# The norms' inverse roots on ScalarE as logarithm and exponential, and a weight cast in quarters between squares

## The chip, the cores and the metric

The kernel runs on one core of a Trainium2 chip. The core has TensorE (matrix products into PSUM), VectorE and GpSimd (elementwise work), ScalarE (activation functions and copies) and SyncE, which here only issues transfers; each engine runs its own list of instructions in order, and they meet through semaphores. The metric is the device time of one execution in microseconds: the median of three runs is 2175.29 us (2175.22 to 2176.02).

## The reference

Two blocks follow each other. The first prepends 16 learned tokens to 256 positions of width 1024 and runs two layers of feed-forward, token mixer and feed-forward, each followed by a layer norm:

```python
def layer_norm(x, g, b):
    mu = jnp.mean(xf, axis=-1, keepdims=True)
    var = jnp.mean(jnp.square(xf - mu), axis=-1, keepdims=True)
    return ((xf - mu) * lax.rsqrt(var + LN_EPS) * g + b)
...
h = layer_norm(h, ln_in_g, ln_in_b)
for l in range(DEPTH):
    h = layer_norm(ALPHA * h + 0.5 * swiglu_ffn(h, ...), ...)
    h = layer_norm(ALPHA * h + token_mix(h, ...), ...)
    h = layer_norm(ALPHA * h + 0.5 * swiglu_ffn(h, ...), ...)
```

`token_mix` joins windowed means, a gated causal convolution with a layer norm inside, and a retention with a group norm per head. The second block takes the result with 256 context positions through two layers whose norms are of another kind:

```python
def rms_norm(x, g):
    y = xf * lax.rsqrt(jnp.mean(xf * xf, axis=-1, keepdims=True) + EPS)
    return y * g
...
x = x + g1 * rms_norm(mixer(modulate(rms_norm(x, g0), ...)), g1n)
x = x + g2 * rms_norm(conv_ffn(modulate(rms_norm(x, g2n), ...)), g3n)
```

Its even layer mixes with a windowed attention and a bidirectional mLSTM, its odd layer with latent attention, whose query and key ranks have an rms_norm each. The context goes through the even layer alone. All of it is float32. Every `rsqrt` here is one of the roots that the change rewrites, but for the one per head in the mLSTM's output (HSTD), which is computed as logarithm and exponential already.

## The kernel before, in words

The activations lie transposed: 128 channels on the partitions, eight tiles of 1024 channels, and positions along the free axis (272 in the first block, 2 x 256 in the second). A weight matrix comes in units of 128x2048 into four slots of a ring (RAW). A product in float32 is made of three products of shorter numbers: the weight is split into a rounded part WHI (`high`, a cast on ScalarE, line 1484) and a remainder WLO (`rest`, a subtraction on VectorE, line 2080), the input likewise into XHI and XLO, or XB and its remainder; TensorE multiplies high by high, low by high and high by low. `high(n)` waits until unit n has landed and its slot's parts are free.

The order of the work on each engine is written out by hand, one function per engine and stage; semaphores with counted values join them. No scheduler reorders it.

A layer norm of the first block runs so. The last output tiles of a feed-forward come out of TensorE one after the other. VectorE adds the residual (PL, line 2162), ScalarE squares (`square_tiles`, SLF, line 1518), VectorE and GpSimd sum squares and tiles, TensorE sums over the channels with a matrix of ones, ScalarE squares the mean (DSQ), VectorE forms the variance (VAR, line 2202), ScalarE takes the square root (RSTD, line 1527), VectorE inverts it (`invert`, line 2132) and scales PL (line 2119), ScalarE writes XHI and X (lines 1492, 1494), VectorE the remainder XLO (line 2126). Meanwhile TensorE runs `keep_busy`: matrix products of ones with no user (fillers in the text). q counts these norms from 0 to 5; q=0, 2, 3 and 5 end a feed-forward (`ffn1`), q=1 and 4 end a mixer. At q=0, 2 and 3 the next stage's second unit is cast on ScalarE behind the root; at q=5 between two squares.

In the second block an input norm squares X (SQ), sums on TensorE (`in_stat`), takes the root into RSTD for the latents or RSC for the context (`in_root`, line 1711), inverts it (`in_recip`, line 2425) and forms PRE and XB (`in_tiles`, lines 2436 and 2441; `in_hi`, line 1716). An output norm (`y_square`, `y_root`, line 1725) ends in `post`, which inverts (line 2461), scales PRE and adds it to X. In the mixers there are CSTD (the convolution's norm, inverted at line 2376) and GSTD (the group norm, line 2395, which TensorE spreads over the partitions); in the odd layer DQSTD and CKSTD (lines 2747 and 2753).

ScalarE holds one set of activation tables at a time. Where the next activation's function isn't in it, an ACT_TABLE_LOAD stands ahead of it; a one-element activation into DUMMY was used to bring a load forward.

Of the kernel before, what the change touches and what calls it, by code (L numbers as in the profile page):

```python
# [20 lines left out]
CT = D // P  # L21
# [50 lines left out]
def build(nc, A, out):  # L72
    with ExitStack() as ctx:
# [40 lines left out]
        DUMMY = small.put("DUMMY", [1])  # L114
# [197 lines left out]
        def conv_at(i, f):  # L312
# [18 lines left out]
        ln_centred, ln_std, ln_rstd, ln_scaled = sem("ln_centred"), sem("ln_std"), sem("ln_rstd"), sem("ln_scaled")  # L331
# [23 lines left out]
        def halves(name):  # L355
            return [sem(f"{name}{z}") for z in range(2)]

        in_sq, norm_power, norm_std, in_scaled, in_high, in_low = (
            halves("in_sq"), halves("norm_power"), halves("norm_std"), halves("in_scaled"), halves("in_high"),
            halves("in_low"))  # L360
# [15 lines left out]
        odd_done, odd_taken, odd_mm, odd_std, odd_step = (  # L376
            sem("odd_done"), sem("odd_taken"), sem("odd_mm"), sem("odd_std"), sem("odd_step"))
# [295 lines left out]
        def _(pe):  # L673
# [141 lines left out]
            def mixer(l):  # L815
# [76 lines left out]
                pe.wait_ge(cv_std, l + 1)  # L892
# [38 lines left out]
                pe.wait_ge(gn_rstd, l + 1)  # L931
# [96 lines left out]
            def even_inputs():  # L1028
# [6 lines left out]
                pe.wait_ge(norm_std[0], in_at(0))  # L1035
                pe.wait_ge(ln_std, 7)
                half_unit(EVEN0 + 2, 0, 4)
                pe.wait_ge(norm_std[1], in_at(0))
# [220 lines left out]
            def ffn_both():  # L1259
# [3 lines left out]
                pe.wait_ge(norm_std[1], in_at(1))  # L1263
# [30 lines left out]
                for z in (1, 0):  # L1294
                    for j in range(CT):
# [8 lines left out]
                        if z == 0 and j == 7:  # L1304
                            pe.wait_ge(norm_std[1], y_at(1))
# [10 lines left out]
            def odd_inputs():  # L1316
# [38 lines left out]
                for n in range(4):  # L1355
# [10 lines left out]
                    if n == 0:  # L1366
                        pe.wait_ge(odd_taken, 2)
                        pe.wait_ge(norm_std[1], in_at(2))
                        mm(pe, PS[:, 3, :], ONES[:, 2, :], CKSQ[:, :], True, True).then_inc(odd_mm, 1)
                        pe.wait_ge(tab_loaded, RT_LOADED)  # L1370
                        pe.wait_ge(odd_std, 1)
# [97 lines left out]
        def _(act):  # L1469
# [15 lines left out]

            def norm_out(e, gain, bias):
# [11 lines left out]
            def input_norm():  # L1498
                act.wait_ge(start_set, N_SET)
                act.activation(DUMMY[:, :], EPS5[:, :], ACT.Sqrt)  # L1500
# [8 lines left out]
                act.activation(RSTD[:, 0:L1], PS[:, 5, 0:L1], ACT.Sqrt, bias=EPS5[:, 0:1]).then_inc(ln_std, 1)  # L1509
# [10 lines left out]
            def norm(q, behind_root=lambda: None):  # L1520
# [6 lines left out]
                act.activation(RSTD[:, tk], VAR[:, tk], ACT.Sqrt, bias=EPSH[:, 0:1]).then_inc(ln_std, 1)  # L1527
                behind_root()
# [9 lines left out]
            def ffn1(l, b):  # L1538
# [42 lines left out]
                act.activation(DUMMY[:, :], EPSH[:, :], ACT.Sqrt)  # L1581
                square_tiles(q, SLF, range(3, 4))
                if q == 5:
                    high(u0 + FFN_STEPS + 1)
                square_tiles(q, SLF, range(4, CT))
                norm(q, (lambda: None) if q == 5 else (lambda: high(u0 + FFN_STEPS + 1)))

            def mixer(l):
# [74 lines left out]
                act.activation(CSTD[:, :], PS[:, 1, 0:L1], ACT.Sqrt, bias=EPS5[:, 0:1]).then_inc(cv_std, 1)  # L1663
# [11 lines left out]
                act.activation(GS[:, 2:4, :], PS[:, 2:4, 0:L1], ACT.Silu).then_inc(gs_done, 1)  # L1675
                act.wait_ge(gn_var, l + 1)
                act.activation(GSTD[:, :], PS[:, 4, 0:L1], ACT.Sqrt, bias=EPS5[:, 0:1]).then_inc(gn_std, 1)
# [1324 lines left out]
```

## Time and profile before

| | us |
|---|---|
| median of three runs (lowest to highest) | 2175.29 (2175.22 to 2176.02) |
| profiled execution: span, first to last instruction | 2171.1 |
| time of the profiled execution outside its span | not listed |
| median of the runs less the span | 4.2 |
| TensorE busy | 2110.9 (97%) |
| VectorE busy | 1571.7 (72%) |
| ScalarE busy | 1054.7 (49%) |
| GpSimd busy | 156.5 (7%) |
| mean granted TensorE clock, share of full speed | 0.994 |

PE is TensorE's matrix products, DVE VectorE, ACT ScalarE, POOL GpSimd. A busy share is an average over stages with different limits; what an edit is worth is read where it stands, from the wait that ends last there. A table load on ScalarE takes 1.283 us, and there are 33.

### The profile page before, as it was taken

What the parts mean: (1) busy time and instruction counts of PE and PEld (TensorE: products, weight loads), DVE (VectorE), ACT (ScalarE), POOL (GpSimd) and SP (SyncE); (2) the same over time, 40 slices, a digit from 0 to 9 for tenths busy, and PEclk for the clock granted to TensorE, in tenths of its full rate; (3) what the DMA queues carried; (4) which work ended last, traced back from release to release, by engine and by line L of the source; (5) the groups of instructions that cost most, each with busy time, mean ns of one, the idle gap of its engine ahead of it and who ended that gap; (6) DMA issues with size and microseconds to landing.
All of it is one profiled execution on the core that took longest, in us unless ns stands there. A gap on an engine that the chain in (4) does not pass through costs nothing.

```text
span 2171.1 us, 35296 instructions
## 1 busy us (share of the span) xinstructions
PE 2110.9 (97%) x14830; PEld 1928.9 (89%) x14830; DVE 1571.7 (72%) x2374; ACT 1054.7 (49%) x1551; POOL 156.5 (7%) x195
## 2 busy tenths in 40 slices
PE   9999999999999999999999988999999999999997
PEld 8999989999999998999897774898888888579997
DVE  7878998878988798998852667466556346858774
ACT  6443656443644465644552446345445234746653
POOL 1201102201200101200100000000000001100000
PEclk9999999999999999999999999999999999999999
DMA  7665526666566543777331120113222222123552
GB/s 293 224 239 191 211 92 262 233 239 248 211 235 245 205 156 119 273 276 254 126 120 54 59 96 9 58 61 117 97 97 96 98 78 100 37 78 118 189 179 97
DMA packets 48334, 334.93 MB, mean 154 GB/s; under 512 B 5612, under 2 KB 6716, under 8 KB 8880
## 3 DMA queue, kind: packets, MB, share of 16 engines
q1 hardware_dynamic: 38384, 267.47, 34.7%
q0 software_dynamic: 9792, 65.21, 8.0%
q8 instruction: 117, 1.92, 0.4%
q14 instruction: 41, 0.34, 0.0%
HBM read 331.61 MB, written 1.05 MB: 153 GB/s over the span
## 4 chain that ended last, share of the span: by engine, by line
PE 84%; DVE 9%; ACT 3%; issue 2%; DMA 1%; POOL 1%; DVEq 0%; ACTq 0%; POOLq 0%
PE PS L468 83%; ACT WHI L1484 1%; PE PS L1214 1%; DVE WLO L2080 1%; DVE PRE L2436 1%; POOL SUM L571 1%; DVE RSTD L2132 1%; DVE XB L2441 0%; DVE STAT L2648 0%; DVE PL L2194 0%; DVE PL L2121 0%; DMA RAW<-in_up_a 0%; DMA RAW<-in_mix 0%; DVE TM L2595 0%; ACT PR L1895 0%
## 5 line engine op out<-in xcount | busy, mean ns | idle before, releaser
L2080 DVE TENSOR_TENSOR WLO<-RAW,WHI 128x2048 fp32r<-128x2048 f32 (+1 forms) x251 | 572.4, 2285 | 214.1 <-ACT WHI L1484 211.4
L468 PE MATMUL PS<-XB,WHI 128*128 128x256 f32 (+1 forms) x3136 | 702.1, 320 | 6.7 <-DVE XB L2441 2.4
L1484 ACT CAST WHI<-RAW 128x2048 fp32r<-128x2048 f32 (+1 forms) x251 | 474.9, 1895 | 283.3 <-DMA RAW<-in_dn_c 78.1
L468 PEld LDWEIGHTS PS<-XB,WHI 128*128 128x128 f32 x3136 | 523.0, 191 | 51.3 <-issue 8.9
L468 PE MATMUL PS<-XHI,WHI 128*128 128x272 f32 (+1 forms) x1760 | 497.9, 289 | 4.2 <-ACT XHI L1492 4.2
L468 PE MATMUL PS<-XB,WLO 128*128 128x256 f32 (+1 forms) x1568 | 498.0, 318 | 0.0
L468 PE MATMUL PS<-XHI,WLO 128*128 128x272 f32 (+1 forms) x1760 | 489.4, 287 | 0.0
L468 PE MATMUL PS<-XLO,WHI 128*128 128x272 f32 (+1 forms) x1760 | 481.2, 287 | 2.3 <-DVE XLO L2126 2.3
L468 PEld LDWEIGHTS PS<-XHI,WHI 128*128 128x128 f32 x1760 | 328.3, 188 | 8.2 <-issue 7.1
L468 PEld LDWEIGHTS PS<-XLO,WHI 128*128 128x128 f32 x1760 | 322.2, 188 | 4.1 <-DVE XLO L2126 3.6
L468 PEld LDWEIGHTS PS<-XHI,WLO 128*128 128x128 f32 x1760 | 325.7, 188 | 0.0
L468 PEld LDWEIGHTS PS<-XB,WLO 128*128 128x128 f32 x1568 | 299.5, 191 | 20.1
L468 PE MATMUL PS<-GHI,WHI 128*128 128x272 f32 (+1 forms) x704 | 200.1, 286 | 0.0
L468 PE MATMUL PS<-GHI,WLO 128*128 128x272 f32 (+1 forms) x704 | 199.7, 285 | 0.0
L2491 DVE SCALAR_TENSOR_TENSOR AC<-CB,FCW,AC 128x512 f32<-128x512 f32 (+1 forms) x176 | 97.1, 614 | 131.5 <-ACT AC L1742 103.8
L468 PE MATMUL PS<-GLO,WHI 128*128 128x272 f32 (+1 forms) x672 | 191.9, 286 | 0.0
L468 PEld LDWEIGHTS PS<-GHI,WLO 128*128 128x128 f32 x704 | 132.5, 188 | 0.0
L468 PEld LDWEIGHTS PS<-GHI,WHI 128*128 128x128 f32 x704 | 132.4, 188 | 0.0
L2109 DVE CUSTOM_DVE_ANT_0 PROD<-AW,SCB,ADAB 128x1024 f32<-128x1024 f32 x96 | 131.4, 1368 | 0.0
L1549 ACT ACTIVATE SG<-PS 128x272 f32<-128x272 f32 (+1 forms) x88 | 34.5, 393 | 196.8 <-PE PS L468 196.4
L2109 DVE CUSTOM_DVE_ANT_0 AW<-AW,SCB,ADAB 128x1024 f32<-128x1024 f32 x96 | 127.1, 1324 | 0.0
L468 PEld LDWEIGHTS PS<-GLO,WHI 128*128 128x128 f32 x672 | 126.4, 188 | 0.0
(376 smaller groups left out, 2516.6 us busy)
## 6 DMA issues: line engine op xcount, KB each, us to landing
AW<-in_ada POOLq DMA_DIRECT2D x48, 1024.0 KB, 7.1
RAW<-in_up_c SPq DMA_DIRECT2D x44, 1024.0 KB, 4.9
RAW<-in_up_a SPq DMA_DIRECT2D x42, 1024.0 KB, 5.1
RAW<-in_up_b SPq DMA_DIRECT2D x42, 1024.0 KB, 5.0
RAW<-in_mix SPq DMA_DIRECT2D x30, 1024.0 KB, 4.9
RAW<-in_dn_a SPq DMA_DIRECT2D x22, 1024.0 KB, 4.9
RAW<-in_dn_b SPq DMA_DIRECT2D x22, 1024.0 KB, 4.9
RAW<-in_dn_c SPq DMA_DIRECT2D x22, 1024.0 KB, 4.9
```

The costliest lines, as they stand in the source:

```text
L468: return pe.matmul(o, w, x, start=first, stop=last)
L571: pool.tensor_tensor(s, PL[:, 0, tk] if j == 1 else s, PL[:, j, tk], ALU.add).then_inc(sum_added, 1)
L1214: last = pe.transpose(PS[:, 4 + e, j * P:(j + 1) * P], probs[e][:, j * P:(j + 1) * P], IDN[:, :])
L1484: act.copy(WHI1[:, s, 0:w], RAW[:, s, 0:w]).then_inc(w1_high, 1)
L1549: act.activation(SG[r, f % 2, tk], PS[r, 2 * (f % 3), tk], ACT.Silu).then_inc(silu1_done, 1)
L2080: v.tensor_tensor(WLO1[:, s, 0:w], RAW[:, s, 0:w], WHI1[:, s, 0:w].bitcast(F32), ALU.subtract)\
L2109: v.tensor_tensor_reduce(PROD[:, :] if g == 0 else w, w, SCB[:, g, :], 1.0, ADAB[:, t:t + 1], ALU.mult, ALU.add, MODF[:, t, g:g + 1]).then ...
L2132: v.reciprocal(RSTD[:, tk], RSTD[:, tk]).then_inc(ln_rstd, 1)
L2436: v.scalar_tensor_tensor(PRE[:, k, HALF[z]], X[:, k, HALF[z]], GIN[:, l, w, k, z:z + 1], rst(z), ALU.mult, ALU.mult).then_inc(in_scaled[z], 1)
L2491: return v.scalar_tensor_tensor(o, i, vec(a, t), o, ALU.mult, ALU.add)
```

## The change

A new helper on ScalarE writes the logarithm of variance plus epsilon in place of the square root, waits for it, and writes the exponential of minus one half of it over it. VectorE's inverses of 128x256 and wider all go, with their waits; their users wait for the exponential. Where TensorE had waited for a root only because its PSUM bank was then read, it waits for the logarithm (`norm_log`, `ln_log`, `cv_log`, `odd_log`). The logarithm and the exponential share a table set, which is loaded by name at chosen places (`roots_ahead`), where before there were loads at each change of function and the DUMMY activations.

At the end of the four feed-forwards of the first block the cast of the next stage's second unit is now made in four pieces of 128x512, one ahead of each of the last four squares. The first piece waits for the unit to land.

```diff
+            def roots_ahead():
+
+                act.preload_act_table_set("natural_log_exp_and_others")
+
+            def inverse_root(o, src, eps, log, log_at, root):
+
+                act.activation(o, src, ACT.Ln, bias=eps[:, 0:1]).then_inc(log, 1)
+                act.wait_ge(log, log_at)
+                act.activation(o, o, ACT.Exp, scale=-0.5).then_inc(root, 1)
+
+            def high_part(n, c):
+
+                s, q = slot_of[n], slice(512 * c, 512 * c + 512)
+                if c == 0:
+                    act.wait_ge(w1_loaded[s], 16 * loads[n])
+                    if earlier[n] is not None:
+                        r, value = released[earlier[n]]
+                        act.wait_ge(r, value)
+                last = act.copy(WHI1[:, s, q], RAW[:, s, q])
+                if c == 3:
+                    last.then_inc(w1_high, 1)
...
-                act.activation(RSTD[:, 0:L1], PS[:, 5, 0:L1], ACT.Sqrt, bias=EPS5[:, 0:1]).then_inc(ln_std, 1)
+                inverse_root(RSTD[:, 0:L1], PS[:, 5, 0:L1], EPS5, ln_log, 1, ln_std)
                 high(1)
...
-                act.activation(RSTD[:, tk], VAR[:, tk], ACT.Sqrt, bias=EPSH[:, 0:1]).then_inc(ln_std, 1)
-                behind_root()
+                inverse_root(RSTD[:, tk], VAR[:, tk], EPSH, ln_log, q + 2, ln_std)
...
                 high(u0 + FFN_STEPS)
                 square_tiles(q, SLF, range(0, 3))
-                act.activation(DUMMY[:, :], EPSH[:, :], ACT.Sqrt)
+                roots_ahead()
                 square_tiles(q, SLF, range(3, 4))
-                if q == 5:
-                    high(u0 + FFN_STEPS + 1)
-                square_tiles(q, SLF, range(4, CT))
-                norm(q, (lambda: None) if q == 5 else (lambda: high(u0 + FFN_STEPS + 1)))
+                for j in range(4, CT):
+                    high_part(u0 + FFN_STEPS + 1, j - 4)
+                    square_tiles(q, SLF, (j,))
+                norm(q)
...
                 act.wait_ge(cv_var, l + 1)
-                act.activation(CSTD[:, :], PS[:, 1, 0:L1], ACT.Sqrt, bias=EPS5[:, 0:1]).then_inc(cv_std, 1)
+                roots_ahead()
+                inverse_root(CSTD[:, :], PS[:, 1, 0:L1], EPS5, cv_log, l + 1, cv_std)
                 high(u0 + 13)
...
                 act.activation(GS[:, 2:4, :], PS[:, 2:4, 0:L1], ACT.Silu).then_inc(gs_done, 1)
+                roots_ahead()
                 act.wait_ge(gn_var, l + 1)
-                act.activation(GSTD[:, :], PS[:, 4, 0:L1], ACT.Sqrt, bias=EPS5[:, 0:1]).then_inc(gn_std, 1)
+                inverse_root(GSTD[:, :], PS[:, 4, 0:L1], EPS5, gn_log, l + 1, gn_std)
                 act.wait_ge(pw_done, l + 1)
...
             def in_root(e, z, bank):
                 act.wait_ge(norm_power[z], in_at(e))
-                act.activation(rst(z), PS[:, bank, 0:SEQ], ACT.Sqrt, bias=EPS6[:, 0:1]).then_inc(norm_std[z], 1)
+                inverse_root(rst(z), PS[:, bank, 0:SEQ], EPS6, norm_log[z], in_at(e), norm_std[z])
...
                 act.wait_ge(norm_power[z], y_at(m))
-                act.activation(rst(z), PS[:, bank, 0:SEQ], ACT.Sqrt, bias=EPS6[:, 0:1]).then_inc(norm_std[z], 1)
+                inverse_root(rst(z), PS[:, bank, 0:SEQ], EPS6, norm_log[z], y_at(m), norm_std[z])
...
                 centre(0)
-                invert(e)
+                v.wait_ge(ln_std, e + 1)
                 scale(0)
...
             def post(m, z):
                 v.wait_ge(norm_std[z], y_at(m))
-                vs.link(v.reciprocal(rst(z), rst(z)))
...
-                in_recip(0, 1)
                 v.wait_ge(ln_out, 8 * 7)
                 in_tiles(0, 1)
                 rest(EVEN0 + 3)
```

`roots_ahead()` is also called ahead of the mLSTM's gate exponential and behind the last gate of both feed-forwards of the second block.

How the instructions stand on ScalarE at the end of the feed-forward before q=2. SLF are the squares, WHI the weight cast, DSQ and RSTD the norm's, XHI and X its outputs. Before:

```order
290 L1581 ACT_TABLE_LOAD
291 L1581 ACTIVATE DUMMY<-EPSH 128x1
292 L1518 ACTIVATE SLF<-PL 128x272 [waits tile_taken] x5
293 L1525 ACTIVATE DSQ<-PS 128x272 [waits ln_mean]
294 L1527 ACTIVATE RSTD<-VAR,EPSH 128x272 [waits ln_var]
295 L1484 CAST WHI_79<-RAW 128x2048 [waits unit1_done,w1_loaded2]
296 L1492 ACTIVATE XHI_66<-PL,VEC 128x272 [waits ln_scaled,vec_loaded]
```

And now:

```order
300 L1487 ACT_TABLE_LOAD
301 L1539 ACTIVATE SLF<-PL 128x272 [waits tile_taken]
302 L1503 CAST WHI_78<-RAW 128x512 [waits unit1_done,w1_loaded2]
303 L1539 ACTIVATE SLF<-PL 128x272 [waits tile_taken]
304 L1503 CAST WHI_78<-RAW 128x512
305 L1539 ACTIVATE SLF<-PL 128x272 [waits tile_taken]
306 L1503 CAST WHI_78<-RAW 128x512
307 L1539 ACTIVATE SLF<-PL 128x272 [waits tile_taken]
308 L1503 CAST WHI_78<-RAW 128x512
309 L1539 ACTIVATE SLF<-PL 128x272 [waits tile_taken]
310 L1546 ACTIVATE DSQ<-PS 128x272 [waits ln_mean]
311 L1491 ACTIVATE RSTD<-VAR,EPSH 128x272 [waits ln_var]
```

The cast has moved from behind the root to between the squares; behind row 311 there follows the exponential, and then XHI.

On ScalarE around the first mixer's group norm (GSTD); the casts from PS behind it are the convolution's output, rounded. Before:

```order
182 L1675 ACTIVATE GS<-PS 128x544 [waits unit1_done]
183 L1677 ACT_TABLE_LOAD
184 L1677 ACTIVATE GSTD<-PS,EPS_60 128x272 [waits gn_var]
185 L1680 CAST XHI_66<-PS 128x272 [waits pw_done]
186 L1680 CAST XHI_66<-PS 128x272
```

And now:

```order
190 L1696 ACTIVATE GS<-PS 128x544 [waits unit1_done]
191 L1487 ACT_TABLE_LOAD
192 L1491 ACTIVATE GSTD<-PS,EPS_60 128x272 [waits gn_var]
193 L1493 ACTIVATE GSTD<-GSTD 128x272 [waits gn_log]
194 L1702 CAST XHI_65<-PS 128x272 [waits pw_done]
195 L1702 CAST XHI_65<-PS 128x272
```

One instruction more, with a wait of ScalarE for its own logarithm, stands ahead of the casts.

On VectorE at the very end: the last sum of squares, and the products that end in the output. Before:

```order
2064 L2455 TENSOR_TENSOR SUMS<-SUMS,SQ 128x512 [waits y_taken1]
2065 L2461 RECIPROCAL RSTD<-RSTD 128x256 [waits norm_std1]
2066 L2471 TENSOR_TENSOR PRE<-PRE,RSTD 128x2x256 [waits vec_step]
2067 L2471 TENSOR_TENSOR PRE<-PRE,RSTD 128x2x256
2068 L2475 TENSOR_TENSOR X<-X,PRE 128x2x256 [waits vec_step]
```

And now:

```order
2039 L2466 TENSOR_TENSOR SUMS<-SUMS,SQ 128x512 [waits y_taken1]
2040 L2481 TENSOR_TENSOR PRE<-PRE,RSTD 128x2x256 [waits norm_std1]
2041 L2481 TENSOR_TENSOR PRE<-PRE,RSTD 128x2x256
2042 L2485 TENSOR_TENSOR X<-X,PRE 128x2x256 [waits vec_step]
2043 L2481 TENSOR_TENSOR PRE<-PRE,RSTD 128x2x256
```

The inverse is gone, and its user waits for ScalarE itself.

## Rows read from the trace of the kernel before

**Rows 1.** The page: busy time, share of the span, instructions.

```profile
PE 2110.9 (97%) x14830; PEld 1928.9 (89%) x14830; DVE 1571.7 (72%) x2374; ACT 1054.7 (49%) x1551; POOL 156.5 (7%) x195
```

**Rows 2.** TensorE's waits by releaser: us in total, times, longest.

```profile
PE PS L468 <- ACT XHI L1492: 4.2, 5, 0.9
...
PE PS L468 <- DVE XLO L2126: 2.3, 6, 0.8
```

**Rows 3.** Groups by line and shape, VectorE: busy us, mean ns | idle before.

```profile
L2132 DVE RECIPROCAL RSTD<-RSTD 128x272 f32<-128x272 f32 x5 | 9.3, 1851 | 0.0
```

**Rows 4.** The same view, ScalarE: the layer norms' root, and a cast of 128x512.

```profile
L1527 ACT ACTIVATE RSTD<-VAR,EPSH 128x272 f32<-128x272 f32 x4 | 2.1, 522 | 2.4 <-DVE VAR L2202 2.4
...
L1781 ACT CAST HFH<-G 128x512 fp32r<-128x512 f32 x3 | 1.8, 605 | 0.0
```

**Rows 5.** Timeline, layer norm q=0: start, duration, what, idle before and its releaser.

```profile
218.15 3.62 PE L468 MATMUL PS<-ONES 128*128 128x256 f32 x16
...
219.45 1.85 DVE L2132 RECIPROCAL RSTD<-RSTD 128x272 f32<-128x272 f32 x1
...
221.87 0.61 ACT L1492 ACTIVATE XHI<-PL,VEC 128x272 fp32r<-128x272 f32 x1 [0.67 <-DVE PL L2119]
...
222.63 0.36 PE L468 MATMUL PS<-XHI,WHI 128*128 128x272 f32 x1 [0.87 <-ACT XHI L1492]
...
223.93 0.76 PE L468 MATMUL PS<-XLO,WHI 128*128 128x272 f32 x4 [0.30 <-DVE XLO L2126]
```

**Rows 6.** Timeline of ScalarE at q=2, the sixth square.

```profile
540.09 0.43 ACT L1518 ACTIVATE SLF<-PL 128x272 f32<-128x272 f32 x1 [0.54 <-DVE PL L2162]
```

**Rows 7.** Timeline of the even layer's softmax, ScalarE and TensorE.

```profile
1326.75 1.28 ACT L1878 ACT_TABLE_LOAD   x1
1328.04 0.69 ACT L1878 ACTIVATE HSTD<-PS,EPS 128x512 f32<-128x512 f32 x1
...
1330.04 0.63 ACT L1881 ACTIVATE HSTD<-HSTD 128x512 f32<-128x512 f32 x1
...
1332.80 1.11 PE L1214 MATMUL PS<-IDN,PR 128*128 128x128 f32 x8 [1.40 <-DVE PR L2657]
```

**Rows 8.** Timeline of TensorE in the even layer's input norms.

```profile
1071.08 3.72 PE L468 MATMUL PS<-SQ,ONES 128*128 128x256 f32 x16 [0.83 <-ACT SQ L1706]
1076.69 0.47 PE L468 MATMUL PS<-XB,WHI 128*128 128x256 f32 x2 [1.90 <-DVE XB L2441]
...
1095.34 0.47 PE L468 MATMUL PS<-XB,WHI 128*128 128x256 f32 x2 [1.14 <-DVE WLO L2080]
```

**Rows 9.** Timeline of the odd layer's input norms, ScalarE and TensorE.

```profile
1801.71 0.47 ACT L1725 ACTIVATE RSC<-PS,EPS 128x256 f32<-128x256 f32 x1 [4.71 <-PE PS L468]
...
1812.54 0.70 PE L468 MATMUL PS<-SQ,ONES 128*128 128x256 f32 x2 [3.02 <-ACT SQ L1706]
...
1827.43 0.92 PE L468 MATMUL PS<-DQSQ,ONES 128*128 128x256 f32 x3 [0.56 <-ACT DQSQ L1990]
```

**Rows 10.** Timeline of TensorE in the odd layer's output.

```profile
1957.78 0.48 PE L468 MATMUL PS<-SQ,ONES 128*128 128x256 f32 x1 [0.55 <-ACT SQ L1706]
```

**Rows 11.** Timeline of the end, ScalarE and VectorE.

```profile
2161.18 0.47 ACT L1725 ACTIVATE RSTD<-PS,EPS 128x256 f32<-128x256 f32 x1 [1.43 <-PE PS L468]
2161.68 1.75 DVE L2461 RECIPROCAL RSTD<-RSTD 128x256 f32<-128x256 f32 x1 [1.73 <-ACT RSTD L1725]
```

**Rows 12.** Timeline of the first mixer, behind the group norm's root.

```profile
314.15 0.79 DVE L2392 TENSOR_TENSOR XLO<-PS,XHI 128x272 fp32r<-128x272 f32 x2 [0.30 <-ACT XHI L1680]
...
315.03 0.36 PE L468 MATMUL PS<-YPH,WHI 128*128 128x272 f32 x1
```

**Rows 13.** Timeline of the latents' feed-forward behind its last gate.

```profile
2097.15 0.70 ACT L1783 CAST XB<-G 128x256 fp32r<-128x256 f32 x2
...
2099.46 0.75 DVE L2523 TENSOR_TENSOR XB<-G,XB 128x256 fp32r<-128x256 f32 x2
```

**Rows 14.** Windows: length, busy us of PE, PEld, DVE, ACT, POOL, clock, DMA share, GB/s.

```profile
1808.00:1818.00 10.00, 6.77 (x30) 5.40 (x28) 7.18 (x13) 2.49 (x4) 0.00 (x0) 0.83 0.01 2
```

More of the change, by code:

```diff
@@ L113, in build @@
         EPSH = small.put("EPSH", [1])
-        DUMMY = small.put("DUMMY", [1])
         X = place("X", "X", 0, [CT, L2])
@@ L356, in halves @@
             return [sem(f"{name}{z}") for z in range(2)]
-        in_sq, norm_power, norm_std, in_scaled, in_high, in_low = (
-            halves("in_sq"), halves("norm_power"), halves("norm_std"), halves("in_scaled"), halves("in_high"),
-            halves("in_low"))
+        in_sq, norm_power, norm_log, norm_std, in_scaled, in_high, in_low = (
+            halves("in_sq"), halves("norm_power"), halves("norm_log"), halves("norm_std"), halves("in_scaled"),
+            halves("in_high"), halves("in_low"))
         y_done, y_squared, y_taken, x_ready = (
@@ L891, in mixer @@
                 pe.wait_ge(cv_centred, l + 1)
-                pe.wait_ge(cv_std, l + 1)
+                pe.wait_ge(cv_log, l + 1)
                 for t in range(2):
@@ L930, in mixer @@
                 out_blocks(2, range(4))
-                pe.wait_ge(gn_rstd, l + 1)
+                pe.wait_ge(gn_std, l + 1)
                 for h in range(RH):
@@ L1034, in even_inputs @@
                 half_pair(EVEN0, 0, 0, 0)
-                pe.wait_ge(norm_std[0], in_at(0))
-                pe.wait_ge(ln_std, 7)
+                pe.wait_ge(norm_log[0], in_at(0))
+                pe.wait_ge(ln_log, 7)
                 half_unit(EVEN0 + 2, 0, 4)
-                pe.wait_ge(norm_std[1], in_at(0))
+                pe.wait_ge(norm_log[1], in_at(0))
                 half_unit(EVEN0 + 3, 0, 6)
@@ L1262, in ffn_both @@
                 in_stat(1, 1, 7)
-                pe.wait_ge(norm_std[1], in_at(1))
+                pe.wait_ge(norm_log[1], in_at(1))
                 half_unit(FFN0 + 3, 0, 6)
@@ L1338, in query_power @@
                     pe.wait_ge(odd_taken, 1)
-                    pe.wait_ge(norm_std[0], y_at(1))
+                    pe.wait_ge(norm_log[0], y_at(1))
                     for t in range(2):
@@ L1518, in square_tiles, with norm @@
                     act.activation(sl[:, j, tk], PL[:, j, tk], ACT.Square).then_inc(tile_squared, 1)
-            def norm(q, behind_root=lambda: None):
+            def norm(q):
                 l, e = q // 3, q % 3
@@ L1812, in even_inputs @@
                         high(EVEN0 + 8)
+                roots_ahead()
                 act.wait_ge(gate_step, GATES_ABS)
@@ L1957, in ffn_both @@
                         hidden_high(0, f - 16)
+                roots_ahead()
                 for d in range(DN_UNITS):
@@ L1991, in odd_inputs @@
                 act.wait_ge(odd_mm, OD_DQ)
-                act.activation(DQSTD[:, :], PS[:, 2, 0:SEQ], ACT.Sqrt, bias=EPS6[:, 0:1]).then_inc(odd_std, 1)
+                inverse_root(DQSTD[:, :], PS[:, 2, 0:SEQ], EPS6, odd_log, 1, odd_std)
                 act.wait_ge(*released[O_DKV])
@@ L1997, in odd_inputs @@
                 act.wait_ge(odd_mm, OD_CK)
-                act.activation(CKSTD[:, :], PS[:, 3, :], ACT.Sqrt, bias=EPS6[:, 0:1]).then_inc(odd_std, 1)
+                inverse_root(CKSTD[:, :], PS[:, 3, :], EPS6, odd_log, 2, odd_std)
                 act.wait_ge(pool2_step, HEADS_ZERO)
@@ L2043, in ffn_latent @@
                         hidden_high(1, f - 16)
+                roots_ahead()
                 for d in range(DN_UNITS):
@@ L2144, in input_norm @@
                     .then_inc(w1_split, 1)
-                invert(0)
+                v.wait_ge(ln_std, 1)
                 v.wait_ge(in_centred, 4)
@@ L2375, in mixer @@
                 v.wait_ge(cv_std, l + 1)
-                v.reciprocal(CSTD[:, :], CSTD[:, :]).then_inc(cv_rstd, 1)
-                v.wait_ge(cv_rstd, l + 1)
                 v.wait_ge(cv_squared, l + 1)
@@ L2393, in mixer @@
                         .then_inc(y_low, 1)
-                v.wait_ge(gn_std, l + 1)
-                v.reciprocal(GSTD[:, :], GSTD[:, :]).then_inc(gn_rstd, 1)
                 for c in range(4):
@@ L2430, in in_tiles @@
                 v.wait_ge(gains_step, 10 * (l + 1))
-                vs.wait()
+                v.wait_ge(norm_std[z], in_at(e))
                 if e:
@@ L2746, in odd_inputs @@
                 v.wait_ge(odd_std, 1)
-                vs.link(v.reciprocal(DQSTD[:, :], DQSTD[:, :]))
                 for t in range(2):
@@ L2751, in odd_inputs @@
                 assert od.n == DQ_AT
-                v.wait_ge(odd_std, 2)
-                vs.did(v.reciprocal(CKSTD[:, :], CKSTD[:, :]))
                 v.wait_ge(odd_mm, OD_KPE)
@@ L2758, in odd_inputs @@
                 assert od.n == KPE_AT
-                vs.wait()
+                v.wait_ge(odd_std, 2)
                 od.link(v.tensor_tensor(CKV[:, :], CKV[:, :], CKSTD[:, :], ALU.mult))
```

36 lines of the change are left out of this document (11 added, 25 removed).

## The prediction

> **What bounds the kernel now.** I read the page's busy shares first. TensorE is busy 2110.9 us of a span of 2171.1 [rows 1], so what the change can give back is at most the time in which TensorE stands idle, plus what lies ahead of its first and behind its last matmul. Next I read TensorE's waits, grouped by what released them: the norms' first rounded tile XHI is waited for 4.2 us in five waits, its remainder XLO 2.3 us in six [rows 2]. Behind each of these stands a root. The durations of the inverse (1.85 us for 128x272 on VectorE) and of ScalarE's instructions come from the groups by line and shape [rows 3, 4]. Then I read the timeline around each place where a root is late, because the groups alone don't say which wait ends last there: several inverses (CSTD, CKSTD) sit in VectorE time that nobody waits for.
>
> **The price of one root.** Before: square root 0.52 on ScalarE, inverse 1.85 on VectorE [rows 3, 4]. After: logarithm, then an exponential in place. The only such pair in the trace is HSTD, 128x512, where logarithm and exponential take 0.69 and 0.63 [rows 7]. For 128x272 I take the root's own 0.52 for the exponential too. A hand-over between engines is 0.03 (the last root ends at 2161.65, its inverse starts at 2161.68) [rows 11]; for the new wait of ScalarE on its own logarithm I take about the same, 0.05. From above it is bounded by HSTD: between the logarithm's end at 1328.73 and the exponential at 1330.04 lie 1.31 us, which hold a table load of 1.28 as well [rows 7]; from below by 0. A root's result is then ready 1.85 + 0.03 - 0.52 - 0.05, some 1.3 us earlier (1.25 for 128x256, where the inverse takes 1.75 and the root 0.47 [rows 11]), and ScalarE is free some 0.5 us later.
>
> **Part by part,** each by its place, as time taken from TensorE's path.
>
> Layer norms of the first block (five of seven inverses at L2132). At q=0 TensorE runs 16 filler matmuls from 218.15 to 221.77, is idle 0.87 until XHI, and 0.30 more until XLO. The chain is root, inverse (219.45 to 221.30), scale, XHI at 221.87 [rows 5]. It becomes 1.3 shorter; but TensorE can't start before its fillers end, so the gain is the two gaps, 1.17, and 0.13 is lost to the fillers. The same gaps to a hundredth stand at q=1, 2 and 3, and 0.99 at q=4: 4 x 1.17 + 0.99 = 5.7. The input norm has one gap of 0.8 at its XLO (the longest in XLO's row [rows 2]); ScalarE's weight cast now queues behind the exponential and ahead of XHI, so I take 0.7.
>
> The quartered cast. Four pieces of 128x512 at 0.6 [rows 4] come to 2.4 us where one piece took 1.9, each placed ahead of a square. At q=2 ScalarE idles 0.54 ahead of the sixth square [rows 6], about as much ahead of the seventh and more ahead of the last; a piece of 0.6 pushes the middle ones by 0.3 to 0.5, the last by nothing. VectorE adds them behind GpSimd's sums, which TensorE waits for anyway, so I put 0.1 on the four ends together; at worst the middle squares' 0.5 reaches the sum at each, 2 us. At the last layer norm (q=5) the whole cast stood between squares and held up the adds; 0.48 goes there, counted next.
>
> The last layer norm and the context's and latents' input norms. Three inverses stand in one chain. TensorE's gaps are 0.83 at 1071.08, 1.90 at 1076.69 and 1.14 at 1095.34 [rows 8]. By the first, 0.48 (the adds) and 0.83 are gained, and thirteen fillers limit more. The second gap shrinks by the context root's 1.4 (the exponential replaces 1.75 and its hand-over, and the chain ahead of it has gained more than the fillers let through). Start of the unit: -2.7. The third waits for a weight remainder WLO which VectorE starts right behind the latents' norm; that norm's inverse was 1.75 of VectorE's time, so VectorE comes 4.4 earlier, against TensorE's 2.7, and the 1.14 goes. Sum 3.9.
>
> mLSTM: two of the table loads (1.28 each) go ahead of its decays; a TensorE gap of 0.35 goes: 0.4. Softmax of the even layer: two table loads go, ahead of HSTD's logarithm and between it and the exponential [rows 7]; the probabilities come over 2 us earlier, and the gap of 1.40 at 1332.80 closes: 1.4. The other gaps of these stages (2.8, 2.1, 1.8) come from softmax chains without a root and stay.
>
> The odd layer's input norms. ScalarE takes the context's output root at 1801.71 and then rounds XB; the exponential pushes XB, and with it VectorE's side, by 0.5. The context root's inverse behind it on VectorE, another 1.75, goes. Squares are ready 1.3 earlier, and of the gap of 3.02 at 1812.54 1.3 goes. The gap of 0.56 at 1827.43 (DQSQ) goes [rows 9], because the chain ahead of it is 2.5 shorter, and 0.48 at DQSTD's inverse: 2.35. Odd output: 0.55 at 1957.78 [rows 10] and one more such gap, 0.53 in front of the next XB, go; both are then limited by fillers: 1.1.
>
> The end. The inverse 2161.68 to 2163.43 lies between the last root and the last products, with no TensorE work beside it [rows 11]: the whole 1.25 is gained.
>
> What it costs. In the two mixers ScalarE takes the group norm's root and, right behind it, rounds the convolution's output; VectorE's remainder follows at 314.15 to 314.94 and TensorE's matmul at 315.03 [rows 12], with a small stretch in that matmul: it has no slack. The exponential comes between: 0.5 each, 1.0. The inverse's own user, TensorE's spread of GSTD, comes later and has slack, as does the convolution's CSTD. Added table loads: one now stands behind the last gate of the latents' feed-forward, ahead of the two casts to XB, whose remainder VectorE begins at 2099.46 [rows 13], behind other work. The casts fill 0.7 and stood 1.6 us ahead of that remainder; 1.28 later they still are ready: nothing. The Trainium skill, page "ScalarE: Activation LUTs", section "What ACT_TABLE_LOAD costs", puts a drain of about 1.38 us on top of each load's 1.28. By it this place would add some 1.0 us and the sum be 14.7. The rows speak against it: the load runs from 1326.75 to 1328.03 and the logarithm starts at 1328.04 [rows 7]; the sum keeps 1.28.
>
> **Sum.** 0.7 + 5.7 + 3.9 + 0.4 + 1.4 + 2.35 + 1.1 + 1.25 = 16.8 gained, 0.1 + 1.0 lost: -15.7. The span becomes 2155.4. The span of before lies 4.2 under the median of the timed runs, 2175.29, and no other time of the profiled execution is given; I carry the 4.2 over: **2159.6 us**, 0.72% faster.
>
> **Rivals.**
>
> A. A next wait takes half. After each root the chain may end in what was just behind it: an XLO that VectorE reaches later, a weight transfer that ends at its old time. For: ScalarE's casts wait for transfers in nearly every stage, and fillers already cut 0.1 to 1.5 off several chains. Against: behind 223.93 TensorE runs without a gap for 30 us, and transfers are issued when TensorE or VectorE frees a slot, so they move along. Half of the sum is 7.9: about 2167.4.
>
> B. The clock gives more. In 1808 to 1818 the granted clock averages 0.83 [rows 14]: a stretch at the lower level, 1.2 GHz, begins at 1813.5, behind the gap of 3.02. Twelve matmuls there take 4.3 us. With the shorter gap TensorE may stay at 2.4 GHz and the squares then set the end, 1.6 earlier. Four other such stretches follow gaps of 1.8 to 2.8 that stay, but one beside a shortened chain may go as well. About 2157. Against: at 1240 a gap of 1.95 was enough.
>
> C. The slower side: ScalarE's wait on its own logarithm. If the exponential starts only after the logarithm has gone through the engine and this costs 1.3 us (the bound above) or more, a root is ready no earlier than with the inverse, while ScalarE is held longer. Then the layer norms, the input norm, the end and odd output give 0, the even inputs some 1.5 (casts and the earlier WLO), softmax and mLSTM 1.8 by their table loads; the mixers lose 2 x 1.8, XB 1.8 and the squares 0.1. That is +2.2 at 1.3, about 2177.5. Between 0.05 and 1.3 the sum moves by 17.9, so it turns at 1.15 us, and passes 4.4 slower at 1.45. Against: the same pair of rows holds a load of 1.28 in a distance of 1.31, and if the load didn't overlap the wait, 0.03 is left.
>
> D. The change doesn't reach the path: only if XHI waited for something beside the root. The chain at q=0 leads through the inverse without a pause, so I give it little: within 4 us of before.
>
> **Chances.** Forecast 0.58, A 0.20, B 0.12, C 0.04, D 0.06. About 0.2% (4.4 us) is what a measurement of this kernel tells from no change. Forecast, A and B all lie beyond it: faster 0.89. D and the milder half of C: same 0.08; slower 0.03. The forecast's own range is 2157 to 2163: the unknown wait may be 0.15 instead of 0.05 at some twelve places that aren't limited by fillers (+1), the squares +2, the clock -2. Taking in A and B, 8 in 10 lie in **2155.5 to 2167.5**.
>
> **What the profile after would show.** No inverse of 128x256 or wider on VectorE; 25 table loads for 33. An exponential of 128x272 of about 0.5 us starting within 0.1 of the logarithm's end (C: over 1 us later). TensorE going from the fillers to XHI without a gap at each layer norm; if a gap of over 0.3 stays there, the chain's sum is wrong. The gap in front of SQ in the odd layer at 1.2 to 1.8 us, and the granted clock behind it tells B. A stall of about 0.5 in each mixer at the YPH matmuls. TensorE's idle time down from some 50 us to some 36. The sum would be wrong above all if gaps reappear a few microseconds behind each norm, at a WLO or XLO (A).

## The result and the profile after

The changed kernel takes 2151.23 us (median of four runs, 2148.96 to 2151.74), the kernel before 2175.26; the ratio is 0.9887, 95% interval 0.9875 to 0.9899. It is 24 us faster, where 15.7 were forecast, and the time lies under the range of 2155.5 to 2167.5. The span of its profile is 2149.9 us, 21.2 less than before.

The page and TensorE's waits of the changed kernel, to be read beside [rows 1, 2]:

```profile
PE 2107.2 (98%) x14830; PEld 1928.9 (90%) x14830; DVE 1523.1 (71%) x2348; ACT 1057.0 (49%) x1577; POOL 155.3 (7%) x195
```

```profile
PE PS L467 <- ACT SQ L1728: 1.7, 3, 1.2
```

The norms' XHI and XLO are gone from the list. VectorE has 26 instructions and 49 us less. ScalarE is no busier: 26 exponentials more, seven table loads less (26 for 33; the prediction had 25).

The price of a root, from the groups by line and shape on ScalarE, and the timeline at q=0, to be read beside [rows 3 to 5]. First the root and its user before, then the changed kernel:

```profile
218.89 0.52 ACT L1527 ACTIVATE RSTD<-VAR,EPSH 128x272 f32<-128x272 f32 x1 [0.61 <-DVE VAR L2202]
...
221.33 0.79 DVE L2119 TENSOR_TENSOR PL<-PL,RSTD 128x272 f32<-128x272 f32 x2
```

```profile
L1493 ACT ACTIVATE RSTD<-RSTD 128x272 f32<-128x272 f32 x5 | 2.1, 430 | 0.2
```

```profile
216.90 3.62 PE L467 MATMUL PS<-ONES 128*128 128x256 f32 x16
...
217.64 0.52 ACT L1491 ACTIVATE RSTD<-VAR,EPSH 128x272 f32<-128x272 f32 x1 [0.61 <-DVE VAR L2221]
218.19 0.43 ACT L1493 ACTIVATE RSTD<-RSTD 128x272 f32<-128x272 f32 x1
218.66 0.79 DVE L2144 TENSOR_TENSOR PL<-PL,RSTD 128x272 f32<-128x272 f32 x2 [0.42 <-ACT RSTD L1493]
...
220.16 0.47 PE L467 MATMUL PS<-XHI,WHI 128*128 128x272 f32 x1
...
221.25 0.77 PE L467 MATMUL PS<-XLO,WHI 128*128 128x272 f32 x4
```

The exponential starts 0.03 behind the logarithm's end and takes 0.43, not 0.52. From the root's start to its user 1.02 us pass; before, 2.44. TensorE goes from the fillers to XHI without a gap, and its first XHI matmul starts at 220.16, 0.36 before the fillers' drawn end at 220.52: the end of a matmul in the profile isn't the point at which the next can start. From the root's start to this matmul 2.52 us pass (3.74 before), to the first XLO matmul 3.61 (5.04 before): TensorE is 1.22 earlier at XHI, which the fillers hold up by some 0.2, and 1.43 earlier at XLO.

The odd layer's input norm and the end, beside [rows 9, 14, 11]:

```profile
1797.42 1.13 PE L467 MATMUL PS<-SQ,ONES 128*128 128x256 f32 x4 [1.22 <-ACT SQ L1728]
```

```profile
1793.00:1803.00 10.00, 8.25 (x51) 6.92 (x50) 7.09 (x16) 3.81 (x8) 0.74 (x1) 1.00 0.01 2
```

```profile
2141.84 0.42 ACT L1493 ACTIVATE RSTD<-RSTD 128x256 f32<-128x256 f32 x1
2142.28 1.29 DVE L2481 TENSOR_TENSOR PRE<-PRE,RSTD 128x512 f32<-128x512 f32 x2 [2.18 <-ACT RSTD L1493]
```

TensorE runs the same 14830 matmuls in the same order in both, so the two traces can be laid over each other: how much earlier (in us) the same matmul starts. By place, against the prediction's terms:

| place | forecast | measured |
|---|---|---|
| input norm | 0.7 | 1.25 |
| layer norms q=0 to 4 | 5.7 | 6.9 |
| ends of the feed-forwards, adds (q=2, 3, 5) | 0.4 | 0.85 |
| the two mixers | -1.0 | -0.6 |
| context's and latents' norms | 3.4 | 4.1 |
| mLSTM, even softmax | 1.8 | 1.85 |
| stretches at the lower clock, mLSTM and softmax | 0 | -0.8 |
| odd layer's input norms | 2.35 | 3.8 |
| odd output | 1.1 | 2.25 |
| the end | 1.25 | 1.35 |
| elsewhere | 0 | 0.25 |
| span | 15.7 | 21.2 |

(The prediction's 3.9 at the last layer norm holds the 0.5 of the adds; they stand in the third line here.)

### The profile page after: what moved, and what is told of

Read it like the earlier page. It is cut to its first block, busy times and chain, and to the rows that moved or that the text cites. A ratio compares the mean times of both kernels' runs of the same rounds, so it can differ in the third digit from the quotient of the medians.

```text
span 2149.9 us, 35296 instructions
## 1 busy us (share of the span) xinstructions
PE 2107.2 (98%) x14830; PEld 1928.9 (90%) x14830; DVE 1523.1 (71%) x2348; ACT 1057.0 (49%) x1577; POOL 155.3 (7%) x195
## 3 DMA queue, kind: packets, MB, share of 16 engines
HBM read 331.61 MB, written 1.05 MB: 155 GB/s over the span
## 4 chain that ended last, share of the span: by engine, by line
PE 89%; DVE 5%; ACT 3%; issue 2%; DMA 0%; POOL 0%; DVEq 0%; ACTq 0%; POOLq 0%
PE PS L467 88%; PE PS L1213 1%; DVE WLO L2105 1%; ACT WHI L1483 1%; DMA RAW<-in_up_b 0%; DVE STAT L2656 0%; POOL SUM L570 0%; DVE TM L2603 0%; DVE AC L2501 0%; PE PS L1130 0%; DVE ACC L2298 0%; DVE TM L2587 0%; DVE PT L2342 0%; ACT PR L1918 0%; DVE XB L2452 0%
## 5 line engine op out<-in xcount | busy, mean ns | idle before, releaser
L1483 ACT CAST WHI<-RAW 128x2048 fp32r<-128x2048 f32 (+1 forms) x247 | 467.2, 1894 | 278.2 <-DMA RAW<-in_dn_c 75.7
```

The lines of the kernel that those rows point to most:

```text
L1483: act.copy(WHI1[:, s, 0:w], RAW[:, s, 0:w]).then_inc(w1_high, 1)
```

## The experiments

**The cast put back, the roots kept.**

```diff
-                for j in range(4, CT):
-                    high_part(u0 + FFN_STEPS + 1, j - 4)
-                    square_tiles(q, SLF, (j,))
-                norm(q)
+                if q == 5:
+                    high(u0 + FFN_STEPS + 1)
+                square_tiles(q, SLF, range(4, CT))
+                norm(q, (lambda: None) if q == 5 else (lambda: high(u0 + FFN_STEPS + 1)))
```

> The changed kernel with the cast of the next stage's second unit put back where it was (whole, behind the root at q=0, 2 and 3, between two squares at q=5). All roots stay as logarithm and exponential. T1 (the roots are the whole gain, the quarters only move work out of the way): behind the root the cast takes 1.9 us on ScalarE, and XHI, which is wanted some 0.6 us after the exponential now, has to wait for it, so 1.3 us are lost at each of three norms and 0.5 at q=5: 2151.2 + 4.4 = 2155.6. T2 (the cast's place doesn't matter because TensorE has slack to its fillers there): within 1 us of 2151.2. What the prediction assumed (quarters cost 0.1 to 2 us): 2149.5 to 2151.

Measured: 2156.78 us, ratio to the kernel before 0.9919 (0.9903 to 0.9935). ScalarE and TensorE at q=0:

```profile
219.81 1.88 ACT L1483 CAST WHI<-RAW 128x2048 fp32r<-128x2048 f32 x1
221.60 0.61 ACT L1513 ACTIVATE XHI<-PL,VEC 128x272 fp32r<-128x272 f32 x1
```

```profile
222.35 0.36 PE L467 MATMUL PS<-XHI,WHI 128*128 128x272 f32 x1 [0.56 <-ACT XHI L1513]
```

XHI starts right behind the cast: what released it isn't the root any more but the engine's own queue. TensorE is 0.98 to 0.99 later at each of q=0, 2 and 3 (T1 had 1.3) and 0.2 at q=5, 3.2 in all by the matmuls' starts. The rest isn't at these places: TensorE gets its full clock 2.6 us later at the start of this profile (1.3 us), and there is one stretch at the lower clock more (up to 1.7). T1 holds.

**The cast alone** (the same edit on the kernel before, with `high_part`).

> The kernel before with the quartered cast alone; square root and inverse stay. T1: only the 0.5 us at q=5 and what TensorE waited for GpSimd's sums at q=2 (0.50) and q=3 (0.28) can go, since behind the root ScalarE waited for the inverse anyway: 2175.3 - 1.2 = 2174.1. T2 (the squares are delayed by the pieces): +0.5 at each of three ends, 2176.5.

Measured: 2175.04 us, 0.9999 (0.9990 to 1.0009), between T1 and T2, neither of which the total rules out. By the matmuls' starts 0.3 us goes at q=5 and nothing at q=0, 2 and 3; the waits for GpSimd's sums don't go as T1 had it (at q=2 the wait is 0.2 longer, at q=3 0.15 shorter). So the quarters are worth next to nothing while the inverse is there, and some 3 us once it has gone. The two edits are not a sum.

**The layer norms' roots alone** (input norm and q=0 to 5, in the kernel before).

```diff
-                act.activation(RSTD[:, tk], VAR[:, tk], ACT.Sqrt, bias=EPSH[:, 0:1]).then_inc(ln_std, 1)
+                inverse_root(RSTD[:, tk], VAR[:, tk], EPSH, ln_log, q + 2, ln_std)
...
-                v.reciprocal(RSTD[:, tk], RSTD[:, tk]).then_inc(ln_rstd, 1)
-                v.wait_ge(ln_rstd, e + 1)
```

> The kernel before with logarithm and exponential in the seven layer norms of the first block alone (input norm, q=0 to 5); the cast, the mixers' norms and all of the second block stay as before. It says how much of the 24 us lies in these seven. By the trace of the changed kernel TensorE comes 1.3 earlier behind the input norm, 1.4 behind each of q=0, 2, 3, 1.0 and 1.3 behind q=1 and 4, and 1.0 at q=5. But the cast stands behind the root here, which costs up to 1.3 at q=0, 2 and 3. T1 (chain-limited, cast in the way): 1.3 + 3 x 0.1 + 2.3 + 1.0 = 4.9 less than before, about 2170.4. T2 (the cast hides): 1.3 + 3 x 1.4 + 2.3 + 1.0 = 8.8 less, about 2166.5.

Measured: 2166.61 us, 0.9969 (0.9953 to 0.9984), 8.5 less, T2's number; but the interval, 3.5 to 10.2 less, holds T1's too. By the matmuls' starts q=0, 2 and 3 give only 0.43 each with the cast behind the root, where T1 had 0.1 and T2 1.4, and the first block gives 7.1 in all, 0.5 of it at the waits for GpSimd's sums. The mechanism is T1's, with 0.3 more at each norm; its profile has one stretch at the lower clock less than that of before (up to 1.7 us).

**The second block alone** (the first put back as before, cast included).

> The changed kernel with the first block put back as before: its layer norms, mixers and the cast have square root, inverse and the old place; the second block keeps logarithm and exponential. T1 (the parts add up but for the cast): with both whole 24.0 is gained, the first block's roots alone gave 8.5, and putting the cast back cost 5.5, which belongs to the first block too: 24.0 - 8.5 - 5.5 = 10.0 less than before, 2165. By the alignment of the two traces: the context's and latents' norms 2.7 + 1.4, softmax 1.6, odd layer 3.8, odd output 2.2, end 1.3 = 13, less what the clock gave: 2162. T2 (the gains of the two blocks overlap): above 2168.

Measured: 2159.43 us, 0.9940 (0.9924 to 0.9957), 15.5 less. That is more than T1's 10 and 13, though the interval (9.4 to 16.5 less) holds both; T2 is out. The matmuls' starts give 12.9 up to the last matmul and 1.3 behind it, with three stretches at the lower clock where before has five. At the context's and latents' norms, the softmax and the odd layer the same matmuls gain what they gain in the changed kernel within 0.3 us: none of the gains overlaps with the first block's.

**The inverses kept, all else changed.**

```diff
-                act.activation(o, o, ACT.Exp, scale=-0.5).then_inc(root, 1)
+                act.activation(o, o, ACT.Exp, scale=0.5).then_inc(root, 1)
...
+                v.reciprocal(RSTD[:, tk], RSTD[:, tk]).then_inc(ln_rstd, 1)
```

> The changed kernel with all of VectorE's inverses kept: logarithm, exponential of plus one half, then the inverse. It computes the same. It keeps the saved table loads and the quartered cast, and each root is later than before by an exponential and a wait (0.46 us). T1 (the inverse's own 1.8 us on the chains is the gain): all of the norms' gain goes and each chain is 0.46 longer at some twelve places (+5.5), while softmax keeps 1.6, mLSTM 0.3 and the adds at q=5 0.5: 2175.1 + 3.1 = 2178. T2 (the table loads and the cast's place carry much of it): 2172 or less.

Measured: 2180.70 us, 1.0029 (1.0017 to 1.0041), 5.7 slower than before. TensorE at q=0:

```profile
223.69 0.36 PE L468 MATMUL PS<-XHI,WHI 128*128 128x272 f32 x1 [1.33 <-ACT XHI L1517]
```

1.33 where [rows 5] has 0.87: the longer chain goes straight into the gap. The saved table loads keep their 1.6 us at the softmax, as T1 had it, and the cast gives nothing at q=0; they don't carry the gain, the inverse's time on the chains does. It is 2.7 slower than T1's 2178: its profile has seven stretches at the lower clock for five, up to 3.4 us.

**One filler call more, and one less,** behind q=0 to 4: `keep_busy(9, 7)` and `keep_busy(7, 7)` for `keep_busy(8, 7)`.

> The changed kernel with one filler call more (two matmuls, 0.45 us by 16 in 3.62) behind each of the five layer norms q=0 to 4. T1 (the chain from the root to XHI ends last; the fillers, whose ends are modelled 0.35 late, have slack of 0.1 to 0.3): +0.15 to 0.35 at each, 0.8 to 1.8 us in all, 2152.0 to 2153.0. T2 (the fillers end last, as the prediction had it): 5 x 0.45 = +2.3, 2153.5.

> The changed kernel with one filler call (two matmuls, 0.45 us) less behind each of q=0 to 4. One more cost 0.19 at each of q=0, 2, 3 and 4 and 0.10 at q=1 by the distance from one norm's sums to the next's. T1 (the fillers have 0.26 of slack against the chain): nothing is gained, 2150.5 to 2151.5, and a gap of 0.2 to 0.4 appears ahead of XHI. T2 (fillers end last): 0.45 less at each, 2.2 in all, 2149.

Measured: 2152.34 (0.9903, 0.9883 to 0.9924) with one more, 2152.79 (0.9903, 0.9888 to 0.9918) with one less. The totals don't separate T1 from T2 here (the intervals are 6 to 9 us wide, and 2152.79 lies above both), the distances do. From the first matmul of q=0's sums (SUM by a matrix of ones, at 214.96) to that of the next sums, in the following stage (at 250.79), TensorE takes 35.83 us in the changed kernel, 36.02 with more fillers and 35.84 with less. At q=4 the same distance is 34.13, 34.10 and 34.14: one call more costs nothing there, not the 0.19 that the second expectation gives. TensorE with one call less:

```profile
217.51 3.19 PE L467 MATMUL PS<-ONES 128*128 128x256 f32 x14
220.56 0.36 PE L467 MATMUL PS<-XHI,WHI 128*128 128x272 f32 x1
...
221.86 0.40 PE L467 MATMUL PS<-XLO,WHI 128*128 128x272 f32 x1 [0.31 <-DVE XLO L2151]
```

XHI starts 0.2 sooner behind the fillers, and the time is lost again at XLO: the gap that T1 put ahead of XHI stands there. The chain ends last, at XLO. A call more costs 0.19 of its 0.43 to 0.45, so the fillers have about 0.25 of slack: T1 in both.

**The chain longer by one logarithm** at q=0 to 4.

```diff
+                if q < 5:
+                    act.activation(DSQ[:, tk], VAR[:, tk], ACT.Ln, bias=EPSH[:, 0:1])
```

> The changed kernel with a second logarithm of the variance, into a scratch tile that nobody reads, ahead of the root at q=0 to 4: the chain from the variance to XHI is longer by ScalarE's issue distance of such an instruction, 0.4 to 0.5 us; nothing else changes. T1 (the chain ends last at every layer norm, without slack): the distance from q=0's sums to the next sums grows from 35.83 by the same 0.4 to 0.5, and the gap that the profile records ahead of XHI is smaller than that, by up to 0.3, since matmuls' ends are modelled. T2 (fillers end last): it grows by less than 0.2, with no gap.

Measured (two runs): 2156.65 us, 0.9914 (0.9885 to 0.9943). The distance grows to 36.23, 36.24, 36.24 and 36.25 at q=0 to 3 (35.82 to 35.83 in the changed kernel), by 0.41, and the recorded gap is 0.29:

```profile
222.55 0.65 PE L467 MATMUL PS<-XLO,WHI 128*128 128x272 f32 x3 [0.29 <-DVE XLO L2153]
```

That is T1, with the gap ahead of XLO and not of XHI. Another 1.05 us were lost at q=2 and 0.87 at q=3, which neither theory had: TensorE waits for GpSimd's sum. At q=2 a cast on ScalarE had waited for a transfer ahead of it.

```profile
530.23 1.91 ACT L1483 CAST WHI<-RAW 128x2048 fp32r<-128x2048 f32 x1 [6.45 <-DMA RAW<-in_up_a]
```

```profile
540.87 0.95 PE L467 MATMUL PS<-SUM,ONES 128*128 128x272 f32 x3 [1.18 <-POOL SUM L570]
```

The transfer was issued at 522.73 and landed at 530.21, 7.5 us; in the changed kernel the same one takes 5.1. In the kernel before, whose TensorE gap at this sum was 0.50, it takes 6.7 and the next one 8.0. Why it is slower isn't shown: an `in_ada` transfer from GpSimd's queue was in flight, but so it was in the changed kernel. Over the profiles the wait at q=2 comes and goes: from q=1's following sums to q=2's it takes 166.05 us in the changed kernel and with the second block alone (whose first block is that of before), 166.42 before, 166.56 with three exponentials later (below) and 167.09 here. So a part of the gain at the feed-forwards' ends (0.5) is timing of this kind and no merit of the edit.

**One inverse kept, DQSTD's.**

```diff
-                inverse_root(DQSTD[:, :], PS[:, 2, 0:SEQ], EPS6, odd_log, 1, odd_std)
+                act.activation(DQSTD[:, :], PS[:, 2, 0:SEQ], ACT.Ln, bias=EPS6[:, 0:1]).then_inc(odd_log, 1)
+                act.wait_ge(odd_log, 1)
+                act.activation(DQSTD[:, :], DQSTD[:, :], ACT.Exp, scale=0.5).then_inc(odd_std, 1)
...
+                vs.link(v.reciprocal(DQSTD[:, :], DQSTD[:, :]))
```

> The changed kernel with VectorE's inverse kept for DQSTD alone (the query rank's norm in the odd layer: logarithm, exponential of plus one half, inverse). It computes the same. The chain there is 1.8 us longer. T1 (a wait costs TensorE 0.2 to 0.3 more than the gap that the profile records, because the last matmul before it is modelled longer than the distance at which the next could start): the place loses g + 0.26, where g is the recorded gap, about 0.95 for a gap of 0.7. T2 (the recorded gap is what it costs): both are equal.

Measured (two runs): 2154.29 us, 0.9903 (0.9874 to 0.9932). TensorE at the first user, here and in the changed kernel:

```profile
1815.46 0.92 PE L467 MATMUL PS<-DQ,RAW 128*128 128x256 f32 x3 [0.93 <-DVE DQ L2755]
```

```profile
1814.40 0.81 PE L467 MATMUL PS<-DQ,RAW 128*128 128x256 f32 x3
```

Ahead of it (the DQSQ sum, 1810.65 and 1810.67) the traces agree within 0.02; the next sum (CKSQ) starts at 1818.16 against 1816.99, 1.19 later. The recorded gap is 0.93. T1: the wait costs 0.26 more than its gap here.

**Three exponentials later,** behind work that is wanted sooner.

```diff
-                inverse_root(GSTD[:, :], PS[:, 4, 0:L1], EPS5, gn_log, l + 1, gn_std)
+                act.activation(GSTD[:, :], PS[:, 4, 0:L1], ACT.Ln, bias=EPS5[:, 0:1]).then_inc(gn_log, 1)
                 act.wait_ge(pw_done, l + 1)
                 for t in range(2):
                     act.copy(XHI1[:, 2 + t, :], PS[:, t, 0:L1]).then_inc(y_high, 1)
+                act.wait_ge(gn_log, l + 1)
+                act.activation(GSTD[:, :], GSTD[:, :], ACT.Exp, scale=-0.5).then_inc(gn_std, 1)
...
                 in_root(2, 1, 1)
-                y_root(1, 0, 2)
+                act.wait_ge(norm_power[0], y_at(1))
+                act.activation(rst(0), PS[:, 2, 0:SEQ], ACT.Ln, bias=EPS6[:, 0:1]).then_inc(norm_log[0], 1)
                 in_hi(2, 1)
+                act.wait_ge(norm_log[0], y_at(1))
+                act.activation(rst(0), rst(0), ACT.Exp, scale=-0.5).then_inc(norm_std[0], 1)
```

> The changed kernel with three exponentials moved behind work that is wanted sooner: both mixers' GSTD behind the two casts of the convolution's output, and the context's output root in the odd layer behind the eight casts to XB (its logarithm stays in front, so the PSUM bank is free). Their users come later. T1 (ScalarE's time in these three places is what TensorE waits for): 0.3 + 0.3 + 0.45 = 1.05 less, 2150.2, and the distance from q=0's sums to q=1's falls from 85.79 by 0.3. T2 (other work takes their place): the same as the changed kernel within 0.3.

Measured: 2149.35 us (2149.20 to 2152.63), 0.9889 (0.9874 to 0.9904).

```profile
311.79 0.68 ACT L1702 CAST XHI<-PS 128x272 fp32r<-128x272 f32 x2
312.36 0.45 ACT L1704 ACTIVATE GSTD<-GSTD 128x272 f32<-128x272 f32 x1
```

From the sums behind q=0 to q=1's (250.79 to 336.58 in the changed kernel) it takes 85.14 for 85.79 us, from those behind q=3 to q=4's 84.15 for 84.40. Of the first 0.65 only 0.3 belongs to the edit: the changed kernel's profile has a wait for GpSimd's sum at q=1, and the other profiles with the same mixer have 85.44 to 85.46. In the odd layer the first XB matmul comes 0.45 earlier. T1 at all three places. It is the fastest of all, but the totals don't separate it from the changed kernel.

**The scatter.** For each profile I summed what the stretches at the lower level (1.2 GHz) cost at most ahead of the last norm, half their length. One costs up to 1.7 us, and most lie in mLSTM and softmax. In the profiles of the second block alone and of the later exponentials these stretches cost up to 5.1 us together, in those of the kernel before and the changed one 8.5, in the kept inverses' 12.0, in the cast's alone 13.6. Over 14 runs the kernel before ranged from 2171.63 to 2179.56. Single totals of these kernels can't be read finer than about 2 us; the distances inside a trace can, to some 0.05, where no wait for GpSimd's sum lies in them; the start, up to the first sums, varies by 1.9 us (48.88 to 50.78).

The two profiles hide a part of this. The granted clock was 0.991 to 0.994 in the 26 runs of the kernel before that were taken beside the experiments, and 0.994 to 0.996 in the four of the changed one. What is missing to 1, times the span, is 16.6 and 10.8 us on average, and 13.3 and 12.8 in the two profiles. By this estimate the changed kernel spends up to some 6 us less on the lower clock, and the pair of profiles shows 0.4 of it. The 24 us of the medians hold more of the clock than the 21.2 of the spans; no run separates how much.

## Why the prediction was wrong

The way, nearly all places and the cause (the roots' chains) were right; the size was not. It gave 15.7 of the span, and 21.2 went; it then added 4.2, and 1.8 was right.

1. The carry-over. "The span of before lies 4.2 under the median ... I carry the 4.2 over" failed. In four runs of the changed kernel the time lies 1.76 to 1.84 above its span, and in 26 of the kernel before 1.75 to 1.85. The profile of before was a quick execution (2171.1 + 1.8 = 2172.9, in a range of 2171.6 to 2179.6), with a granted clock of 0.994 where most runs have 0.992. This alone makes 2.4 us of the miss of 8.4; 5.5 are the span's, below, and 0.5 is the changed kernel's profile, slower than its median.

2. "TensorE can't start before its fillers end, so the gain is the two gaps." Wrong. I took the fillers' drawn end as a bound, and the gaps as the loss. At q=0 the chain became 1.42 shorter (2.44 to 1.02), and TensorE came 1.43 earlier at XLO: all of it. The fillers hold up the first XHI matmul by 0.2, but the wait for XLO behind it takes that back. The filler and chain experiments show it from both sides. The same error sits in each term that was read off a gap: 0.56 at DQSQ was worth 0.83, 0.48 at DQSTD 0.74, 1.40 at softmax 1.61, 1.14 at WLO 1.37. By the table this is 1.2 us at q=0 to 4, 0.7 at the context's and latents' norms, 0.2 at the softmax and 0.5 at DQSQ and DQSTD, some 2.6 together. The page agrees: TensorE's busy time fell by 3.7 us (2110.9 to 2107.2) with the same matmuls, time that no gap had shown; 0.8 of it is point 5's.

3. The exponential's price, 0.43 for 0.52, was mis-sized by 0.09 on each chain; the wait on the logarithm, 0.03 for 0.05, was right, and rival C with it out. The mixers lost 0.3 each at YPH for the 0.5.

4. The odd layer's input norms, 3.8 for 2.35. Here rival B came true, which I had at 0.12. The gap of 3.02 became 1.22, and the stretch at 1.2 GHz behind it is gone: 1.35 at the gap and the XB ahead of it (1.8 less 0.45) for the 1.3, 0.9 for the stretch, and 0.83 and 0.74 for the 0.56 and 0.48 at DQSQ and DQSTD. Over all profiles the four kernels that keep the long gap have it (0.83 over 10 us: before, cast alone, first block's roots, kept inverses), and the eight with a gap of 1.2 don't (1.00). The row of one of the four, the first block's roots, to be read beside that of the changed kernel above:

```profile
1801.00:1811.00 10.00, 6.71 (x27) 4.95 (x25) 6.09 (x14) 2.97 (x5) 0.49 (x1) 0.83 0.01 2
```

That the shorter gap is the cause is likely, not shown: elsewhere gaps of the same size were followed by a stretch (1.33 us at q=3 with the inverses kept, 1.23 at 1906 with DQSTD's). In the changed kernel's profile a stretch at 1240 is gone too and two others came (at 1182 and 1288), so the sum at the lower clock, up to 8.5 us, is the same in both profiles; 0.8 was lost again there.

5. Odd output, 2.25 for 1.1. Behind the gap of 0.55 the sixteen sums took 4.40 us, paced by ScalarE's squares, which wait for VectorE's X; now 3.62, the pace of TensorE. The squares come no faster than before, but earlier against TensorE. I had read the gap and not the pace behind it.

6. The cast. That it costs some 0.1 was right. Its worth, 3 us in the changed kernel, isn't in the sum: I had priced the chains as if ScalarE were free behind the root, which only the quarters make true. A is refuted in general: no gap of over 0.31 reappears behind a norm. In small it is there, in the transfers at q=2 and 3 and at q=1, where a sum now waits 0.2. D is refuted. The drain of about 1.38 us that the Trainium skill, page "ScalarE: Activation LUTs", section "What ACT_TABLE_LOAD costs", puts on a switch of sets would have put the forecast at 14.7 saved and made the miss larger. The changed kernel's trace doesn't show it either: the load at 208.91 takes 1.28 us, and the next square starts at 210.20.

The range was too narrow by its own terms: it held the unknown wait, the squares and the clock, but neither a gap's hidden part (point 2) nor the scatter of one profiled execution, which was the base of the sum.

## What to carry to other kernels

Price a chain that is made shorter by the chain, from the start of its first changed instruction to the start of its user, and not by the recorded gap of the engine that waits; fillers bound it only where no later wait on the same chain takes back what they hold up. In this kernel an inverse root whose result is waited for was worth moving to one engine as logarithm and exponential in one table set (1.02 us for 2.44 from its start to its user), and of that 1.43 some 1.0 came at q=0, 2 and 3 only because the cast queued behind it was moved in the same step. Before a span is turned into a time, compare it with several runs of the same kernel.

## What the runs showed of the hardware

- A dependent exponential starts 0.03 us behind its logarithm; a 128x272 costs 0.43 on ScalarE, while VectorE's inverse of it costs 1.85.
- At DQSTD's user a wait cost TensorE 0.26 us more than the gap in the profile says (1.19 for 0.93).
- At the odd layer's input norm a TensorE pause of 3.0 us was followed by a stretch at 1.2 GHz in four profiles of four, one of 1.2 us in none of eight; elsewhere pauses of 1.33 and 1.23 us were followed by one in a single profile each.
- The same 1 MB transfer took 5.1 us in one profile, 6.7 and 7.5 in others, for a reason not shown, and TensorE met it as a wait for GpSimd of up to 1.2 us.
- A table load took 1.28 us, and the next activation started 0.01 us behind it.
